# Sliding-window attention: where the softmax is scaled, and which operand stands in TensorE

## The chip, the core and the metric

One core of a Trainium2 chip runs the whole kernel as one program. TensorE (PE) multiplies, VectorE (DVE) and ScalarE (ACT) empty PSUM and do the elementwise work, GpSimd (POOL) and the queue of SyncE (SP) do little but issue transfers and small steps. The metric is the device time of one execution in microseconds (us), the median of several runs. Before the change it is 1330.35 us (three runs, 1329.46 to 1332.42).

## What is computed

A decoder trunk of two layers for 256 tokens of width 1024. Layer 0 is a gated linear recurrence and a dense feed-forward; layer 1 is attention over shared keys and values, then eight experts of which each token uses two. The change touches the attention alone:

```
scores = einsum('bnqkgd,bnskd->bnkgqs', qb, k_band) * (64 ** -0.5)
logits = where(valid, scores + bias, -inf)
m      = maximum(max(logits), sink)
p      = exp(logits - m)
probs  = p / (sum(p) + exp(sink - m))
out    = einsum('bnkgqs,bnskd->bnqkgd', probs, v_band).reshape(B, S, 16 * 64)
return out @ w_o
```

There are 16 query heads in 4 groups; the 4 heads of a group share one key head and one value head of width 64. The window is 128 tokens, and the 256 tokens are two tiles of 128: the rows of tile 0 look at the 128 keys of tile 0, those of tile 1 at all 256 keys, with the mask in the bias.

## The kernel before

Each engine has one hand-written program, and semaphores tie them together; an instruction that waits holds up all behind it on its engine. Weights of the dense parts pass through a ring of chunks: ACT rounds a chunk to `w_hi` (L597), DVE takes the rest `w_lo` (L887), and PE forms each product from three fp32r matmuls (L1413 to L1415). The experts run afterwards in a loop of 8 items on PE (L1852, L1864) whose weights come by DMA; its first buffers are loaded as chunk slots come free, and the rest is asked for (L451, L459) when the output projection of the attention has ended.

The attention stage works group by group, g = 0 to 3. Everything that PE turns or that passes from one form to another goes through the two `turn` banks of PSUM, strictly in turn: use n of a bank waits until use n-2 has been read (`turn_bank`). For a group the steps are:

- `logits(g)`, PE: the bias of the group by three 512-column matmuls (L1653), then eight score matmuls (L1708).
- `largest(g)`, DVE: three maxima over PSUM (L1222, L1224) and three small steps, which give `negm`.
- the exponentials, ACT: four of 128 columns (L809), four of 256 columns (L812), each with its row sum in `rsum`, and the sink (L815). The unscaled probabilities of a group are the 12 blocks of 128x128 of `pr`; groups take turns in two such tiles.
- `normalise(g)`, DVE: sum plus sink, reciprocal, and two multiplications that scale all 12 blocks in place (L1235, L1238).
- `turn_probs(g)`, PE: 12 transposes (L1728) in three uses u of a turn bank, each copied by DVE to `pT` (L926).
- `attend(g)`, PE: 12 fp32 matmuls in one use of a turn bank (L1740 to L1742). The values stand (128x64) and the turned probabilities stream, 128 columns. The even head of a pair writes the upper 64 partitions of the bank, the odd one the lower 64. The result has features on the partitions, as the output projection wants it.
- `att_round(g)` on ACT (L798) and `att_rest(g)` on DVE (L1242) split that bank to `ht_hi` and `ht_lo`.
- `project_out(i)`, PE: 24 fp32r matmuls of 512 columns with group i's rows of the output weights, for i = 0 and 1; `finish_out` does i = 2 and 3 bank by bank at the end.

An fp32 matmul has two records in the trace (so the 12 matmuls of `attend` are 24), a transpose and an fp32r matmul one. The order on PE is: logits(0), logits(1), then for each g: turn_probs(g), logits(g+2), attend(g); project_out(0) follows attend(2), project_out(1) stands between turn_probs(3) and attend(3), finish_out follows attend(3). On DVE: largest(0), normalise(0), largest(1), then for each g: the three copies, normalise(g+1), largest(g+2), att_rest(g); the splits of weight chunks C_O+2 and C_O+3 stand inside g = 3.

Of the kernel before, what the change touches and what calls it, by code (L numbers as in the profile page):

```python
# [8 lines left out]
P = 128  # L9
# [3 lines left out]
TT = T // P  # L13
HEADS, HD = 8, 128
CH = 64
NCH = T // CH
QH, KVH, AD = 16, 4, 64
GRP = QH // KVH
# [20 lines left out]
C_O = C_V + N_V  # L39
# [41 lines left out]
def build_program(nc, a, out):  # L81
    f32, f32r = mybir.dt.float32, mybir.dt.float32r
    i32, u32 = mybir.dt.int32, mybir.dt.uint32
    ALU, ACT, AX = mybir.AluOpType, mybir.ActivationFunctionType, mybir.AxisListType
    MUL, ADD, SUB = ALU.mult, ALU.add, ALU.subtract
# [40 lines left out]
    with ctx:  # L126
# [8 lines left out]
        h = sb(ctx, "h", [P, TT, D])  # L135
# [5 lines left out]
        xs = sb(ctx, "xs", [P, TT, D])  # L141
# [249 lines left out]
        HGRN_OUT = [[banks[2], banks[3]], [banks[0], banks[1]]]  # L391
        OUT_BANKS = [[banks[2], banks[3]], [banks[0], banks[4]]]

        TURN_ATT = 3 + HEADS + 4 + TT + 4 + 4 * KVH

        GROUPS = ((0, 0), (0, 1), (1, 0), (1, 1))
        FRESH_1 = [banks[4], banks[5], banks[2], banks[3]]
# [184 lines left out]
        def _(act):  # L582
            own = [0]
            nxt = [0]
            ta = [0]
# [207 lines left out]

            def att_round(g):

                use = ta[0] + 4 * g + 3
                act.wait_ge(turned, use + 1)
                nc.scalar.activation(ht_hi[:, 2 * g:2 * g + 2, :],  # L798
                                     turn[use % 2][:, :].rearrange("p (k t) -> p k t", k=2), ACT.Copy).then_inc(turn_hi, 1)

            for g in range(KVH):
                if g >= 2:

                    att_round(g - 2)
                act.wait_ge(negm_ready, g + 1)
                pr = prs[g % 2]
                l = LOGIT_BANKS[g % 2]
                for hh in range(GRP):
                    nc.scalar.activation(pr[:, hh, :], l[0][:, P * hh:P * hh + P], ACT.Exp, bias=negm[:, g, 0, hh:hh + 1],  # L809
                                         accum_out=rsum[:, g, 0, hh:hh + 1])  # L810
                for hh in range(GRP):
                    ins = nc.scalar.activation(pr[:, 4 + 2 * hh:6 + 2 * hh, :].rearrange("p k c -> p (k c)"),  # L812
                                               l[1 + hh % 2][:, 256 * (hh // 2):256 * (hh // 2) + 256], ACT.Exp,
                                               bias=negm[:, g, 1, hh:hh + 1], accum_out=rsum[:, g, 1, hh:hh + 1])
                nc.scalar.activation(sinkd[:, g, :, :], sinkd[:, g, :, :], ACT.Exp).then_inc(exps_ready, 1)  # L815
                if g == 0:

                    act.wait_ge(chunk_used, C_V + 1)
                    for t in range(TT):
                        nc.scalar.activation(vt[:, t, :], banks[1][:, 256 * t:256 * t + 256], ACT.Copy,  # L820
                                             scale=tok_rstd[:, 2, t:t + 1]).then_inc(kv_out, 1)
            att_round(KVH - 2)
            round_to(C_O + 3)
            att_round(KVH - 1)
            ta[0] += 4 * KVH
            assert ta[0] == TURN_ATT
            round_to(C_MOE - 1)

# [45 lines left out]
        def _(dve):  # L874
# [14 lines left out]
            def rest_to(c_last):  # L889
                while nxt[0] <= c_last:  # L890
                    c = nxt[0]
                    rest_chunk(c, c % RAW, c % SPLIT)
                    nxt[0] += 1
# [26 lines left out]
            def turn_copy(dst, part=None):  # L920

                dve.wait_ge(turned, td[0] + 1)
                src = turn[td[0] % 2][:, :] if part is None else turn[td[0] % 2][:, 0:part]
                if len(dst.shape) == 3:
                    src = src.rearrange("p (a b) -> p a b", a=dst.shape[1])
                nc.vector.tensor_copy(dst, src).then_inc(turn_free, 1)  # L926
                td[0] += 1
# [290 lines left out]
            def largest(g):  # L1218
                l = LOGIT_BANKS[g % 2]
                for i in (1, 0):  # L1220
                    dve.wait_ge(logits_full, 3 * g + 2 - i)
                    then(nc.vector.reduce_max(mx[:, g, 1, i:GRP:2], l[1 + i][:, :].rearrange("p (h k) -> p h k", h=2), axis=AX.X))  # L1222
                dve.wait_ge(logits_full, 3 * g + 3)
                then(nc.vector.reduce_max(mx[:, g, 0, :], l[0][:, :].rearrange("p (h k) -> p h k", h=4), axis=AX.X))  # L1224
                snk = sink[:, GRP * g:GRP * g + GRP].unsqueeze(1).to_broadcast([P, TT, GRP])
                then(nc.vector.tensor_tensor(mx[:, g, :, :], mx[:, g, :, :], snk, ALU.max))
                nc.vector.tensor_tensor(sinkd[:, g, :, :], snk, mx[:, g, :, :], SUB)
                nc.vector.tensor_scalar(negm[:, g, :, :], mx[:, g, :, :], -1.0, None, MUL).then_inc(negm_ready, 1)

            def normalise(g):  # L1230
                pr = prs[g % 2]
                dve.wait_ge(exps_ready, g + 1)
                then(nc.vector.tensor_tensor(rsum[:, g, :, :], rsum[:, g, :, :], sinkd[:, g, :, :], ADD))
                then(nc.vector.reciprocal(rsum[:, g, :, :], rsum[:, g, :, :]))
                nc.vector.tensor_tensor(pr[:, 0:4, :], pr[:, 0:4, :], rsum[:, g, 0, :].unsqueeze(2).to_broadcast([P, 4, P]),  # L1235
                                        MUL).then_inc(probs_ready, 1)
                p1 = pr[:, 4:12, :].rearrange("p (h k) c -> p h (k c)", k=2)
                nc.vector.tensor_tensor(p1, p1, rsum[:, g, 1, :].unsqueeze(2).to_broadcast([P, 4, 2 * P]), MUL).then_inc(probs_ready, 1)  # L1238

            def att_rest(g):  # L1240
                dve.wait_ge(turn_hi, rounded[0] + 1)
                nc.vector.tensor_tensor(ht_lo[:, 2 * g:2 * g + 2, :], turn[td[0] % 2][:, :].rearrange("p (k t) -> p k t", k=2),  # L1242
                                        plain(ht_hi[:, 2 * g:2 * g + 2, :]), SUB).then_inc(turn_free, 1)
                rounded[0] += 1
                td[0] += 1
# [2 lines left out]
            for t in range(TT):  # L1248
                turn_copy(aqT[:, 4:8, P * t:P * t + P])
            rest_to(C_O + 1)  # L1250
            normalise(0)
            largest(1)
            for g in range(KVH):
                if g == KVH - 1:
                    rest_to(C_O + 2)
                for u in range(3):
                    turn_copy(pTs[g % 2][:, 4 * u:4 * u + 4, :])
                if g + 1 < KVH:
                    normalise(g + 1)
                if g + 2 < KVH:  # L1260
                    largest(g + 2)
                if g == KVH - 1:
                    rest_to(C_O + 3)
                att_rest(g)
            rest_to(C_MOE - 1)
            add = lambda t, half: add_part(C_MOE - 1, 6, (t, half), OUT_BANKS[t][half], None)
            add(0, 0)
# [139 lines left out]
        def _(pe):  # L1407
# [315 lines left out]
            def turn_probs(g):  # L1723
                for u in range(3):
                    bank = turn_bank()
                    pe.wait_ge(probs_ready, 2 * g + (1 if u == 0 else 2))
                    for k in range(4):
                        ins = nc.tensor.transpose(bank[:, P * k:P * k + P], prs[g % 2][:, 4 * u + k, :], ident)  # L1728
                    ins.then_inc(turned, 1)
                return tp[0]  # L1730

            def attend(g, turned_by):
                pT = pTs[g % 2]
                pe.wait_ge(turn_free, turned_by)
                bank = turn_bank()
                for hh in range(GRP):
                    row, at = AD * (hh % 2), 256 * (hh // 2)
                    v = [vt[:, t, AD * g:AD * g + AD] for t in range(TT)]
                    d = bank[row:row + AD, at:at + 2 * P]
                    nc.tensor.matmul(d[:, 0:P], v[0], pT[:, hh, :], start=True, stop=True)  # L1740
                    nc.tensor.matmul(d[:, P:2 * P], v[0], pT[:, 4 + 2 * hh, :], start=True, stop=False)
                    ins = nc.tensor.matmul(d[:, P:2 * P], v[1], pT[:, 5 + 2 * hh, :], start=False, stop=True)  # L1742
                ins.then_inc(turned, 1)

            pe.wait_ge(bias_loaded, 16)
            logits(0)
            turn_queries(1)
# [4 lines left out]
            def project_out(i):  # L1752

                pe.wait_ge(turn_free, attended[i])
                to_rows(C_O + i, D, 2, 2 * i, KT, ht_hi, ht_lo, lambda t, q: OUT_BANKS[t][q][:, :], None, "parts")

            for g in range(KVH):
                turned_by = turn_probs(g)

                if g + 2 < KVH:  # L1760
                    logits(g + 2)
                if g == KVH - 1:
                    project_out(1)
                attend(g, turned_by)
                attended.append(tp[0])
                if g == KVH - 2:

                    pe.wait_ge(exps_ready, KVH)
                    project_out(0)
            assert tp[0] == TURN_ATT  # L1770

            def finish_out(t, q):
# [154 lines left out]
```

## Time and profile before

| what | value |
|---|---|
| median of the runs | 1330.35 us |
| profiled execution, its own time | 1331.27 us |
| its span, first to last instruction | 1329.3 us |
| PE busy | 1304.2 us, 98% |
| DVE busy | 360.2 us, 27% |
| ACT busy | 246.3 us, 19% |
| chain of work that ended last | PE 91%, DVE 3%, DMA 3%, ACT 2% |
| mean granted clock of TensorE | 0.995 |

The profiled execution lies 0.92 us above the median, and 1.97 us of its time lie outside the span. PE is busy nearly always, but a busy PE is not one at its peak, so what counts is how long PE takes from one step to the next: the start of a step's first record to the start of the next step's. The attention stage runs from 383 to 427 us of the span, the expert loop from 448.5 to 1321.

### The profile page before, as it was taken

What the parts mean: (1) busy time and instruction counts of PE and PEld (TensorE: products, weight loads), DVE (VectorE), ACT (ScalarE), POOL (GpSimd) and SP (SyncE); (2) the same over time, 40 slices, a digit from 0 to 9 for tenths busy, and PEclk for the clock granted to TensorE, in tenths of its full rate; (3) what the DMA queues carried; (4) which work ended last, traced back from release to release, by engine and by line L of the source; (5) the groups of instructions that cost most, each with busy time, mean ns of one, the idle gap of its engine ahead of it and who ended that gap; (6) DMA issues with size and microseconds to landing.
All of it is one profiled execution on the core that took longest, in us unless ns stands there. A gap on an engine that the chain in (4) does not pass through costs nothing.

```text
span 1329.3 us, 32581 instructions
## 1 busy us (share of the span) xinstructions
PE 1304.2 (98%) x14658; PEld 744.4 (56%) x14658; DVE 360.2 (27%) x539; ACT 246.3 (19%) x370; POOL 55.9 (4%) x50
## 2 busy tenths in 40 slices
PE   9999999999899999999999999999999999999998
PEld 8998899988767434523523533443452353353244
DVE  5875655554875411001001101101100110110111
ACT  5554544433743100000000000000000000000000
POOL 1001000000000230000000000000000000001500
PEclk9999999999999899999999999999999999999999
DMA  9867565555521897999999999999999999999996
GB/s 319 267 213 224 182 191 190 182 199 190 191 96 64 348 421 298 405 409 382 419 421 403 419 420 408 415 420 412 412 418 419 404 419 419 405 418 418 418 417 243
DMA packets 114199, 442.52 MB, mean 333 GB/s; under 512 B 9284, under 2 KB 55700, under 8 KB 83348
## 3 DMA queue, kind: packets, MB, share of 16 engines
q1 hardware_dynamic: 107904, 424.75, 81.4%
q10 hardware_dynamic: 4820, 11.53, 2.5%
q0 software_dynamic: 1344, 4.20, 0.8%
q8 instruction: 120, 1.97, 0.6%
q14 instruction: 11, 0.09, 0.0%
HBM read 434.12 MB, written 12.08 MB: 336 GB/s over the span
## 4 chain that ended last, share of the span: by engine, by line
PE 91%; DVE 3%; DMA 3%; ACT 2%; issue 1%; SPq 0%; ACTq 0%; DVEq 0%
PE bank L1852 41%; PE bank L1864 22%; PE bank L1413 8%; PE bank L1415 8%; PE bank L1414 8%; DMA raw<-in_moe_w_up 2%; DMA dn<-in_moe_w_down 1%; PE bank L1653 1%; PE bank L1571 1%; DVE w_lo L887 1%; ACT w_hi L597 0%; PE bank L1829 0%; DMA const<-in_shape_constants 0%; ACT ht_hi L625 0%; PE bank L1708 0%
## 5 line engine op out<-in xcount | busy, mean ns | idle before, releaser
L1852 PE MATMUL bank<-raw,xT 128*32 128x512 f32 (+1 forms) x4608 | 439.8, 540 | 2.8 <-DMA raw<-in_moe_w_up 2.2
L1852 PEld LDWEIGHTS bank<-raw,xT 128*32 128x32 f32 x4608 | 141.6, 110 | 294.2 <-issue 285.8
L1864 PE MATMUL bank<-dn,hidT 128*32 128x256 f32 x5376 | 291.5, 379 | 1.2 <-DMA dn<-in_moe_w_down 1.2
L1864 PEld LDWEIGHTS bank<-dn,hidT 128*32 128x32 f32 x5376 | 165.8, 110 | 127.4 <-issue 2.8
L1382 DVE TENSOR_TENSOR e_hid<-e_silu,bank 128x512 f32<-128x512 f32 (+1 forms) x48 | 26.9, 616 | 538.0 <-PE bank L1852 538.0
L887 DVE TENSOR_TENSOR w_lo<-raw,w_hi 128x2048 fp32r<-128x2048 f32 x62 | 141.7, 2291 | 102.2 <-ACT w_hi L597 102.1
L1852 PE MATMUL bank<-up_more,xT 128*32 128x384 f32 (+1 forms) x1536 | 150.0, 539 | 0.0
L1413 PE MATMUL bank<-ht_hi,w_hi 128*128 128x256 f32 x464 | 130.1, 280 | 1.5 <-DVE ht_lo L901 1.5
L1414 PE MATMUL bank<-ht_lo,w_hi 128*128 128x256 f32 x464 | 129.8, 280 | 0.0
L1415 PE MATMUL bank<-ht_hi,w_lo 128*128 128x256 f32 x464 | 129.8, 280 | 0.0
L597 ACT ACTIVATE w_hi<-raw 128x2048 fp32r<-128x2048 f32 x62 | 118.6, 1916 | 42.1 <-PE bank L1415 41.8
L860 ACT ACTIVATE e_silu<-bank 128x512 f32<-128x512 f32 (+1 forms) x48 | 22.6, 544 | 433.3 <-PE bank L1852 433.3
L1852 PEld LDWEIGHTS bank<-up_more,xT 128*32 128x32 f32 x1536 | 47.3, 110 | 97.0 <-issue 95.9
L1414 PEld LDWEIGHTS bank<-ht_lo,w_hi 128*128 128x128 f32 x464 | 88.5, 191 | 0.0
L1413 PEld LDWEIGHTS bank<-ht_hi,w_hi 128*128 128x128 f32 x464 | 87.1, 188 | 2.5 <-issue 2.4
L1415 PEld LDWEIGHTS bank<-ht_hi,w_lo 128*128 128x128 f32 x464 | 87.1, 188 | 0.0
L863 ACT ACTIVATE yb<-bank 96x512 f32<-96x512 f32 x8 | 4.7, 593 | 404.7 <-PE bank L1864 404.7
L1413 PE MATMUL bank<-w_hi,ht_hi 128*128 128x256 f32 (+1 forms) x224 | 74.8, 334 | 3.7 <-DVE ht_lo L915 1.6
L1394 DVE COPY yb<-bank 96x256 f32<-96x256 f32 x8 | 3.4, 420 | 257.8 <-PE bank L1864 257.8
L1415 PE MATMUL bank<-w_hi,ht_lo 128*128 128x256 f32 (+1 forms) x224 | 73.2, 327 | 0.0
L1414 PE MATMUL bank<-w_lo,ht_hi 128*128 128x256 f32 (+1 forms) x224 | 73.2, 327 | 0.0
L1413 PEld LDWEIGHTS bank<-w_hi,ht_hi 128*128 128x128 f32 x224 | 42.2, 188 | 9.4 <-issue 3.5
(280 smaller groups left out, 859.5 us busy)
## 6 DMA issues: line engine op xcount, KB each, us to landing
dn<-in_moe_w_down SPq DMA_DIRECT2D x112, 1024.0 KB, 12.5
raw<-in_moe_w_gate SPq DMA_DIRECT2D x48, 1024.0 KB, 14.3
raw<-in_moe_w_up SPq DMA_DIRECT2D x48, 1024.0 KB, 14.4
raw<-in_moe_w_gate SPq DMA_DIRECT2D x48, 768.0 KB, 12.1
raw<-in_moe_w_up SPq DMA_DIRECT2D x48, 768.0 KB, 8.4
up_more<-in_moe_w_gate SPq DMA_DIRECT2D x16, 1024.0 KB, 24.9
up_more<-in_moe_w_up SPq DMA_DIRECT2D x16, 1024.0 KB, 14.1
raw<-in_hgrn_w_in SPq DMA_DIRECT2D x15, 1024.0 KB, 11.7
```

Source lines behind the costliest of these rows:

```text
L597: nc.scalar.activation(w_hi[:, slot, :], raw[:, slot_raw, :], ACT.Copy).then_inc(hi_ready, 1)
L860: nc.scalar.activation(e_silu[:, j, 0:w], banks[j][:, 0:w], ACT.Silu).then_inc(e_silu_ready, 1)
L863: nc.scalar.activation(yb[:, 0:512], banks[6][0:CAP, :], ACT.Copy)
L887: nc.vector.tensor_tensor(w_lo[:, slot, :], raw[:, slot_raw, :], plain(w_hi[:, slot, :]), SUB).then_inc(split_ready, 1)
L1382: nc.vector.tensor_tensor(e_hid[:, j, 0:w], e_silu[:, j, 0:w], banks[GRPS + j][:, 0:w], MUL).then_inc(e_hid_ready, 1)
L1413: nc.tensor.matmul(dst, st[0], mv[0], start=first, stop=False)
L1414: nc.tensor.matmul(dst, st[0], mv[1], start=False, stop=False)
L1415: return nc.tensor.matmul(dst, st[1], mv[0], start=False, stop=last)
L1571: whole = lambda bank_rows, at, w, st, mv: nc.tensor.matmul(bank[bank_rows:bank_rows + CH, at:at + w], st, mv, start=True, stop=True)
L1653: nc.tensor.matmul(LOGIT_BANKS[g % 2][b][:, :], const[:, K_ANTI:K_ANTI + P], bias_rev[:, GRP * g:GRP * g + GRP, :][:, heads, 2 * P - P * ( ...
L1852: ins = nc.tensor.matmul(out_banks[j][GTOK * c:GTOK * c + GTOK, 0:w], xT[:, j, kt, :], chunk[:, c], start=kt == 0, stop=kt == KT - 1)
L1864: ins = nc.tensor.matmul(banks[6 + j // 2][GTOK * c:GTOK * c + GTOK, 256 * (j % 2):256 * (j % 2) + 256], hidT[sup][:, g, m, :], dn[:, i % ...
```

## The change

The probabilities are turned as they come from the exponential. `normalise` is gone from DVE; `sums(g)` keeps its two small steps. In `attend` the operands change places: each block of `pT` (128x128) stands and the values (64 columns) stream over it, so that tokens come out on the partitions: columns 256t + 64h of the bank hold token tile t and head h. `scale_rows(g)` on DVE reads this bank, multiplies it by the reciprocal sums and writes `xs`. A new PE step `turn_heads(g)` turns these rows, four 128x128 transposes in a turn bank of their own, and `att_round` and `att_rest` then split that bank as before. A group so takes five uses of the turn banks and not four. ACT tells PE of its exponentials in three parts (`probs_ready`). The order of the steps is written out anew on PE and DVE; project_out(0) now stands between turn_probs(3) and attend(3), and project_out(1) between turn_heads(2) and turn_heads(3).

```diff
--- before.py
+++ after.py
@@ -391,7 +391,8 @@
...
-        TURN_ATT = 3 + HEADS + 4 + TT + 4 + 4 * KVH
+        PROBS_TURN, HEADS_TURN, ROWS_TURN = (0, 4, 9, 14), (3, 8, 13, 17), (7, 12, 18, 19)
+        TURN_ATT = 3 + HEADS + 4 + TT + 4 + 5 * KVH
@@ -793,25 +794,29 @@
...
-    use = ta[0] + 4 * g + 3
+    use = ta[0] + ROWS_TURN[g]
     act.wait_ge(turned, use + 1)
...
 for g in range(KVH):
-    if g >= 2:
-
-        att_round(g - 2)
+    if g == 2:
+        act.wait_ge(turned, ta[0] + PROBS_TURN[0] + 3)
+    if g == 3:
+        att_round(0)
     act.wait_ge(negm_ready, g + 1)
...
     for hh in range(GRP):
-        nc.scalar.activation(pr[:, hh, :], l[0][:, P * hh:P * hh + P], ACT.Exp, bias=negm[:, g, 0, hh:hh + 1],
-                             accum_out=rsum[:, g, 0, hh:hh + 1])
+        ins = nc.scalar.activation(pr[:, hh, :], l[0][:, P * hh:P * hh + P], ACT.Exp, bias=negm[:, g, 0, hh:hh + 1],
+                                   accum_out=rsum[:, g, 0, hh:hh + 1])
+    ins.then_inc(probs_ready, 1)
     for hh in range(GRP):
...
                                    bias=negm[:, g, 1, hh:hh + 1], accum_out=rsum[:, g, 1, hh:hh + 1])
+        if hh % 2:
+            ins.then_inc(probs_ready, 1)
     nc.scalar.activation(sinkd[:, g, :, :], sinkd[:, g, :, :], ACT.Exp).then_inc(exps_ready, 1)
@@ -819,10 +824,11 @@
...
                                  scale=tok_rstd[:, 2, t:t + 1]).then_inc(kv_out, 1)
-att_round(KVH - 2)
+att_round(1)
 round_to(C_O + 3)
-att_round(KVH - 1)
-ta[0] += 4 * KVH
+att_round(2)
+att_round(3)
+ta[0] += 5 * KVH
 assert ta[0] == TURN_ATT
@@ -1227,15 +1233,22 @@
...
-def normalise(g):
-    pr = prs[g % 2]
+def sums(g):
     dve.wait_ge(exps_ready, g + 1)
...
     then(nc.vector.reciprocal(rsum[:, g, :, :], rsum[:, g, :, :]))
-    nc.vector.tensor_tensor(pr[:, 0:4, :], pr[:, 0:4, :], rsum[:, g, 0, :].unsqueeze(2).to_broadcast([P, 4, P]),
-                            MUL).then_inc(probs_ready, 1)
-    p1 = pr[:, 4:12, :].rearrange("p (h k) c -> p h (k c)", k=2)
-    nc.vector.tensor_tensor(p1, p1, rsum[:, g, 1, :].unsqueeze(2).to_broadcast([P, 4, 2 * P]), MUL).then_inc(probs_ready, 1)
+
+def scale_rows(g):
+
+    dve.wait_ge(turned, td[0] + 1)
+    nc.vector.tensor_tensor(xs[:, :, 256 * g:256 * g + 256].rearrange("p t (h e) -> p t h e", e=AD),
+                            turn[td[0] % 2][:, :].rearrange("p (t h e) -> p t h e", t=TT, e=AD),
+                            rsum[:, g, :, :].unsqueeze(3).to_broadcast([P, TT, GRP, AD]), MUL).then_inc(turn_free, 1)
+    td[0] += 1
+
+def turn_probs_copies(g):
+    for u in range(3):
+        turn_copy(pTs[g % 2][:, 4 * u:4 * u + 4, :])
@@ -1248,20 +1261,27 @@
...
 rest_to(C_O + 1)
-normalise(0)
 largest(1)
-for g in range(KVH):
-    if g == KVH - 1:
-        rest_to(C_O + 2)
-    for u in range(3):
-        turn_copy(pTs[g % 2][:, 4 * u:4 * u + 4, :])
-    if g + 1 < KVH:
-        normalise(g + 1)
-    if g + 2 < KVH:
-        largest(g + 2)
-    if g == KVH - 1:
-        rest_to(C_O + 3)
-    att_rest(g)
+turn_probs_copies(0)
+sums(0)
+largest(2)
+scale_rows(0)
+turn_probs_copies(1)
+sums(1)
+att_rest(0)
+largest(3)
+scale_rows(1)
+turn_probs_copies(2)
+sums(2)
+att_rest(1)
+scale_rows(2)
+turn_probs_copies(3)
+sums(3)
+rest_to(C_O + 2)
+scale_rows(3)
+att_rest(2)
+rest_to(C_O + 3)
+att_rest(3)
 rest_to(C_MOE - 1)
@@ -1723,7 +1743,7 @@
...
         bank = turn_bank()
-        pe.wait_ge(probs_ready, 2 * g + (1 if u == 0 else 2))
+        pe.wait_ge(probs_ready, 3 * g + u + 1)
         for k in range(4):
@@ -1734,14 +1754,21 @@
...
     for hh in range(GRP):
-        row, at = AD * (hh % 2), 256 * (hh // 2)
         v = [vt[:, t, AD * g:AD * g + AD] for t in range(TT)]
-        d = bank[row:row + AD, at:at + 2 * P]
-        nc.tensor.matmul(d[:, 0:P], v[0], pT[:, hh, :], start=True, stop=True)
-        nc.tensor.matmul(d[:, P:2 * P], v[0], pT[:, 4 + 2 * hh, :], start=True, stop=False)
-        ins = nc.tensor.matmul(d[:, P:2 * P], v[1], pT[:, 5 + 2 * hh, :], start=False, stop=True)
+        d0, d1 = (bank[:, 256 * t + AD * hh:256 * t + AD * hh + AD] for t in range(TT))
+        nc.tensor.matmul(d0, pT[:, hh, :], v[0], start=True, stop=True)
+        nc.tensor.matmul(d1, pT[:, 4 + 2 * hh, :], v[0], start=True, stop=False)
+        ins = nc.tensor.matmul(d1, pT[:, 5 + 2 * hh, :], v[1], start=False, stop=True)
     ins.then_inc(turned, 1)
-
+    scaled.append(tp[0])
+
+def turn_heads(g):
+
+    pe.wait_ge(turn_free, scaled[g])
+    turn_rows(lambda t: xs[:, t, :], [g])
+    attended.append(tp[0])
+
+scaled = []
 pe.wait_ge(bias_loaded, 16)
@@ -1754,19 +1781,23 @@
...
-for g in range(KVH):
-    turned_by = turn_probs(g)
-
-    if g + 2 < KVH:
-        logits(g + 2)
-    if g == KVH - 1:
-        project_out(1)
-    attend(g, turned_by)
-    attended.append(tp[0])
-    if g == KVH - 2:
-
-        pe.wait_ge(exps_ready, KVH)
-        project_out(0)
+turned_by = turn_probs(0)
+logits(2)
+attend(0, turned_by)
+turned_by = turn_probs(1)
+turn_heads(0)
+logits(3)
+attend(1, turned_by)
+turned_by = turn_probs(2)
+turn_heads(1)
+attend(2, turned_by)
+turned_by = turn_probs(3)
+pe.wait_ge(exps_ready, KVH)
+project_out(0)
+attend(3, turned_by)
+turn_heads(2)
+project_out(1)
+turn_heads(3)
 assert tp[0] == TURN_ATT
```

## Rows read from the trace of the kernel before

**Rows 1.** Stretches: each engine's busy us, PEclk, DMA share, GB/s.

```profile
core 0: us, PE busy (x) PEld busy (x) DVE busy (x) ACT busy (x) POOL busy (x), PEclk, DMA share, GB/s
383.00:427.00 44.00, 38.96 (x255) 29.43 (x254) 29.04 (x49) 16.38 (x57) 0.00 (x0) 0.96 0.14 49
...
440.00:449.00 9.00, 8.07 (x62) 4.17 (x65) 4.57 (x25) 0.06 (x1) 0.00 (x0) 0.50 1.01 424
449.00:1321.00 872.00, 868.59 (x11522) 354.65 (x11514) 73.80 (x150) 33.79 (x73) 40.25 (x28) 1.00 0.99 405
```

**Rows 2.** Chain that ended last, one item of the expert loop: start, us, what.

```profile
882.94 72.16 PE bank L1852 x768
955.10 36.26 PE bank L1864 x672
```

**Rows 3.** Timeline of SP's queue: start, us, issued transfers.

```profile
436.10 0.81 SPq L451 DMA_DIRECT2D up_more<-in_moe_w_gate  x2
```

**Rows 4.** Waits from 383 to 427 us: total us, times, longest us.

```profile
PE bank L1728 <- DVE pT L926: 2.2, 2, 1.8
PE bank L1728 <- DVE ht_lo L1242: 2.1, 2, 1.2
...
PE bank L1740 <- DVE pT L926: 0.8, 1, 0.8
```

**Rows 5.** Timeline of PE: start, us, line, out<-in, records [idle before <-releaser].

```profile
390.62 0.43 PE L1740 MATMUL bank<-pT,vt 128*64 128x128 f32 x2
...
392.35 0.66 PE L1728 MATMUL bank<-const,pr 128*128 128x128 f32 x4
394.25 1.25 PE L1728 MATMUL bank<-const,pr 128*128 128x128 f32 x8 [1.24 <-DVE ht_lo L1242]
395.34 2.74 PE L1653 MATMUL bank<-bias_rev,const 128*128 128x512 f32 x6
...
399.52 0.43 PE L1740 MATMUL bank<-pT,vt 128*64 128x128 f32 x2
...
401.25 0.66 PE L1728 MATMUL bank<-const,pr 128*128 128x128 f32 x4
...
404.77 0.43 PE L1740 MATMUL bank<-pT,vt 128*64 128x128 f32 x2 [0.78 <-DVE pT L926]
...
407.61 0.80 PE L1413 MATMUL bank<-w_hi,ht_hi 128*128 128x512 f32 x1
...
413.80 1.03 PE L1728 MATMUL bank<-const,pr 128*128 128x128 f32 x8
...
415.59 0.48 PE L1413 MATMUL bank<-w_hi,ht_hi 128*128 128x512 f32 x1
...
421.28 0.43 PE L1740 MATMUL bank<-pT,vt 128*64 128x128 f32 x2
...
423.01 0.50 PE L1413 MATMUL bank<-w_hi,ht_hi 128*128 128x512 f32 x1
```

**Rows 6.** Stretches of 1 us, PE alone: busy, PEclk, DMA share, GB/s.

```profile
406.00:407.00 1.00, 1.00 (x12) 0.50 0.06 16
```

**Rows 7.** Timeline of PE, the router's matmuls: 128x128 stands, 8 columns stream.

```profile
436.84 2.78 PE L1800 MATMUL bank<-router,hnT 128*128 128x8 f32 x24
```

**Rows 8.** Timeline of DVE: start, us, line, operation, operands [idle before].

```profile
371.39 0.69 DVE L1205 TENSOR_TENSOR xs<-bank,rstd 128x512 f32<-128x512 f32 x1
...
389.24 0.69 DVE L1235 TENSOR_TENSOR pr<-pr,rsum 128x512 f32<-128x512 f32 x1
389.85 1.22 DVE L1238 TENSOR_TENSOR pr<-pr,rsum 128x1024 f32<-128x1024 f32 x1
...
393.51 0.69 DVE L1242 TENSOR_TENSOR ht_lo<-bank,ht_hi 128x512 fp32r<-128x512 f32 x1
394.11 0.68 DVE L926 COPY pT<-bank 128x512 f32<-128x512 f32 x1
394.94 0.69 DVE L926 COPY pT<-bank 128x512 f32<-128x512 f32 x1 [0.15 <-PE bank L1728]
```

**Rows 9.** Timeline of ACT: the last exponential of group 3.

```profile
405.12 0.24 ACT L815 ACTIVATE sinkd<-sinkd 128x8 f32<-128x8 f32 x1
```

## Prediction

> **What bounds the kernel now.** I read the stretches first. From 449 to 1321 us, the expert loop, PE is busy 868.59 of 872 us at full clock with the DMA engines at 0.99 [rows 1]; one item of the loop is 72.16 + 36.26 = 108.4 us of the chain with PE in every part of it [rows 2]. The two are nearly tied there, but neither has slack towards the attention: the loop's bulk transfers are asked for at 436.10 us, when the output projection has ended [rows 3], and PE enters the loop behind the same projection. So whatever the attention stage gains or loses shifts both by the same amount, and the whole of it shows in the time. The question is only how long PE takes from 383 to about 427 us.
>
> In that stage PE is busy 38.96 of 44 us [rows 1], so 5.04 us are idle. The waits say to whom: 2.2 us to the copies of `pT` before transposes, 2.1 us to `att_rest`, 0.8 us to a copy before `attend` [rows 4]. That is all that a lighter DVE can give back. The largest piece, 1.8 us, lies in turn_probs(0), where the copy stands behind largest(1); the change leaves this order as it is, so that piece stays. The reader is to see in the timeline of PE that every other step stands directly behind the one before.
>
> **The clock.** From about 405.3 to 408.6 us the granted clock is 0.50, the lower of the two levels, 1.2 GHz [rows 6]; before it fell PE had mostly turned blocks and waited. What it costs is read from equal steps: `attend` takes 392.35 - 390.62 = 1.73 us, and also 1.73 us at 399.52 and at 421.28, but 407.61 - 404.77 = 2.84 us for group 2; project_out(0) takes 413.80 - 407.61 = 6.19 us, project_out(1) 421.28 - 415.59 = 5.69 us [rows 5]. That is 1.1 + 0.5 = 1.6 us.
>
> **Parts with next to no price.** `normalise` gives DVE back 1.8 us a group (389.24 to 389.85 + 1.22) and `scale_rows` takes 0.6 to 0.7 us of it, as a step on a PSUM bank times a broadcast column does [rows 8]. DVE was late for PE only through largest(1) and `att_rest`, so its 4.5 us of lighter work buy only what the walk below shows. The exponentials of group 3 end at 405.4 us now [rows 9]; PE will want them after 408.6, so the finer `probs_ready` buys nothing. `largest` and the split chunks keep their distance: the split of C_O+3 moves behind att_rest(2), 4 us before finish_out needs it, and the queue of SP behind it loads into an idle stretch (DMA share 0.14 [rows 1]).
>
> **The attend step, the term that decides.** Now 24 records in 1.73 us, 72 ns each [rows 5]; the even and odd heads go to different halves of the array's columns. After the change 24 records each put a full 128x128 block in place for 64 columns. No row has that shape; the ends are these. Upper: the router's matmuls stand 128x128 and stream only 8 columns, and 24 records take 2.78 us, of which the last is its own latency of 0.26: (2.78 - 0.26)/23 = 110 ns [rows 7]. There is nothing to stream, so 110 ns is the standing block itself. Lower: if the block could be hidden, 64 columns at half of what the 128 of today's form cost per lane (two lanes, 2 x 55 ns a record) give 55 ns, 1.3 us in all. The router row has the very stationary shape and is nearest, so I take 24 x 0.110 = 2.64 and 0.06 for changing over: 2.70 us. It is +0.97 us for each of four groups, +3.9.
>
> The Trainium skill speaks against this edit: TensorEngine Tiling (Array Packing), section Performance Considerations, advises for a streamed side of 64 or less to swap the operands and tile the columns, which is the form of before, not the one after. TensorE: Matmul & The Clock Gate, section LDWEIGHTS, says that loading takes time by the number of columns, P/1.2 ns, so an estimate of 107 ns for 128; by that the attend step would be 2.6 us, and the 110 ns of the router row agree.
>
> **The walk.** Hand-overs, from group 1 of before: DVE step to PE's next use of its bank 0.74 us (393.51 to 394.25), four transposes with copy behind them 0.69 (394.25 to 394.94), DVE step to next 0.60 (393.51 to 394.11) [rows 5, 8]; four transposes 0.45.
> - Group 1: the first four transposes may start at once; the second four wait for scale_rows(0), which starts 0.2 us after attend's last start plus its latency; then the third, then turn_heads(0), which waits for the copy of the second: 0.92 + 0.69 + 0.74 + 0.48 = 2.83 us until logits(3). Before: 395.34 - 392.35 = 2.99. So -0.2, with the new transposes in it.
> - Group 2 in the same way, ending on the last copy: 2.94 us until attend(2). Before: 404.77 - 401.25 = 3.52. -0.6.
> - Group 3: 0.92 + 0.60 + 0.46 = 1.98 us until the projection; before 415.59 - 413.80 = 1.79. +0.2.
> - turn_heads(2) and (3) stand bare between PE's other work: 2 x 0.44 = +0.9. Their split banks follow at the same distance as now behind attend(3); I add 0.1 for the wait before i = 3.
>
> Sum: 3.9 - 0.2 - 0.6 + 0.2 + 0.9 + 0.1 = +4.3 us, at the same clock on both sides. So the change turns 2 us of waiting into work, and adds more work than that. Against the profiled execution it is 1331.27 + 4.3 = 1335.6; this lies 0.92 above the median, so the forecast for the median is 1330.35 + 4.3 = 1334.6 us.
>
> **The rivals.**
> - The low clock does not come back. For it: group 2's waits shrink. Against: in the new order 64-column records keep the array streaming only half of the time, and three groups of transposes follow each. 1334.6 - 1.6 = 1333.0.
> - It comes back and stays twice as long, since what follows is thin too: +1.6, 1336.3.
> - The standing block is partly hidden: a record of 72 ns, the step stays at 1.73, 1334.6 - 3.9 = 1330.7. Against it stands [rows 7].
> - Faster: records priced by their 64 columns, 55 ns, `attend` 1.3 us (-0.4 each, -1.6 in all), and the clock stays up: 0.4 for the rest of the walk, - 1.6 - 1.6 = -2.8, 1327.5. Its place is the attend step. It decides for faster by over 0.2% where that step takes less than 1.36 us with the clock up; with the clock as before the step would have to be under 0.96. A rule of the skill goes this way: the tiling page's Key Properties say that changing the tiling mode drains the array, and before it changes twice a group. The row shows 1.73 - 1.31 = 0.42 us beyond 24 x 55 ns, which may be that drain; by it alone each step would win at most 0.4.
> - The DVE relief reaches the path after all (the 1.8 us of turn_probs(0) goes): 1332.8. Only if the copies passed largest(1); the written order excludes it.
>
> **How the numbers follow.** A measurement of this kernel can tell about 0.2% from no change, 2.7 us: 1327.7 to 1333.0. Chances: forecast 0.48; clock stays up 0.20; two low stretches 0.12; block partly hidden or some of DVE's relief seen 0.14; faster 0.06. Slower by over 0.2% is the first, the third and part of the second, 0.66; within, 0.27; faster, 0.07. The range leaves out the fast rival and half of the partly hidden one below, and what goes beyond two low stretches above: 1330.6 to 1337.2.
>
> **What would show it.** In the profile after: 24 records of `attend` at 110 ns, 2.6 to 2.8 us a step (0.055 or 0.072 would sink the forecast); four transposes a group more; waits of PE on `xs` of 0.4 us a group in place of those on `ht_lo`; the 1.8 us before turn_probs(0)'s third part still there; project_out(1) at 5.7 us; the loop's items at 108.4 us and its first transfers as much later than 436.1 as the whole kernel is. A low clock at another length than 3.3 us moves the sum by half of the difference.

## The result and the profile after

The change makes the kernel slower by 0.2 to 0.35%: 1332.26 us median (12 runs, 1329.62 to 1334.91) against 1329.38 for the kernel before on the same chip (12 runs). The medians lie 2.9 us or 0.22% apart; the ratio on record for the same runs, with its 95% interval, is 1.0035 (1.0022 to 1.0048). A second comparison later gave 1332.11 against 1329.33 and 1.0020 (1.0007 to 1.0032). The profiled execution took 1334.33 us, its span 1332.5.

The first view is the head of the page of the kernel after: DVE does 5 us less than before, PE 4 us more, and the share that PE is busy is what it was.

```profile
span 1332.5 us, 32618 instructions
...
PE 1308.3 (98%) x14674; PEld 748.9 (56%) x14674; DVE 355.4 (27%) x535; ACT 246.3 (18%) x370; POOL 56.0 (4%) x50
```

The timeline of PE through the stage answers to [rows 5] (start, us, line, operands, records, idle before). One goes from the start of one step to that of the next: the transposes are L1748, attend L1759 to L1761, the bias matmuls L1673, the turned heads L1452, the projection L1433.

```profile
382.11 1.09 PE L1748 MATMUL bank<-const,pr 128*128 128x128 f32 x8
...
389.72 0.43 PE L1759 MATMUL bank<-vt,pT 128*128 128x64 f32 x2
...
392.45 0.61 PE L1748 MATMUL bank<-const,pr 128*128 128x128 f32 x4
393.39 1.25 PE L1748 MATMUL bank<-const,pr 128*128 128x128 f32 x8 [0.34 <-DVE xs L1244]
394.93 0.63 PE L1452 MATMUL bank<-const,xs 128*128 128x128 f32 x4 [0.28 <-DVE pT L932]
395.39 2.74 PE L1673 MATMUL bank<-bias_rev,const 128*128 128x512 f32 x6
...
405.37 0.41 PE L1759 MATMUL bank<-vt,pT 128*128 128x64 f32 x2
...
408.07 0.60 PE L1748 MATMUL bank<-const,pr 128*128 128x128 f32 x4
...
424.21 0.60 PE L1452 MATMUL bank<-const,xs 128*128 128x128 f32 x4
424.56 0.48 PE L1433 MATMUL bank<-w_hi,ht_hi 128*128 128x512 f32 x1
```

An attend step is 392.45 - 389.72 = 2.73 us, and 2.70 for group 2, where the step of before is 1.73 at full clock. The waits of PE in the stage are these (total us, times, longest us); they answer to [rows 4]:

```profile
PE bank L1748 <- DVE pT L932: 1.8, 1, 1.8
PE bank L1748 <- DVE xs L1244: 1.0, 3, 0.3
PE bank L1452 <- DVE pT L932: 0.6, 2, 0.3
```

So 3.4 us of waiting are left of 5.1; the 1.8 us of turn_probs(0) stand untouched.

**Comparing stages, not traces.** The stage did not begin at the same time in any two executions: turn_probs(0) started between 381.1 and 386.7 us in the twelve traces read here, and at 382.11 and 384.56 us in the two of the changed kernel. So I take the stage's own length, from the start of turn_probs(0) to the start of finish_out. It is 424.56 - 382.11 = 42.45 us after, and 423.01 - 383.02 = 39.99 before, of which 1.6 are low clock. Behind the stage both kernels run alike: the bulk transfers are asked for at 437.82 us and not at 436.10 [rows 3], 1.72 us later, and the last addition of the output starts 1.70 us later (1327.80 against 1326.10). The spans differ by more, 3.2 us: the other 1.5 us lie behind that addition, where the span ends 4.7 us after its start in this trace and 3.2 in the first of before. That tail does not go with the kernel: in the second traces it is 3.1 us after the change and 3.6 before it. An item of the expert loop takes 72.16 + 36.26 us in the chain of both [rows 2].

### The profile page after: what moved, and what is told of

Same layout as the page of the kernel before. It is cut to its first block, busy times and chain, and to the rows that moved or that the text cites. A ratio compares the mean times of both kernels' runs of the same rounds, so it can differ in the third digit from the quotient of the medians.

```text
span 1332.5 us, 32618 instructions
## 1 busy us (share of the span) xinstructions
PE 1308.3 (98%) x14674; PEld 748.9 (56%) x14674; DVE 355.4 (27%) x535; ACT 246.3 (18%) x370; POOL 56.0 (4%) x50
## 4 chain that ended last, share of the span: by engine, by line
PE 91%; DMA 3%; DVE 3%; ACT 2%; issue 1%; SPq 0%; ACTq 0%; DVEq 0%
PE bank L1883 41%; PE bank L1895 22%; PE bank L1433 8%; PE bank L1435 8%; PE bank L1434 8%; DMA raw<-in_moe_w_up 2%; DMA dn<-in_moe_w_down 1%; PE bank L1673 1%; PE bank L1591 1%; DVE w_lo L893 1%; ACT w_hi L598 0%; PE bank L1728 0%; PE bank L1860 0%; DMA const<-in_shape_constants 0%; ACT ht_hi L626 0%
## 5 line engine op out<-in xcount | busy, mean ns | idle before, releaser
L1433 PE MATMUL bank<-ht_hi,w_hi 128*128 128x256 f32 x464 | 130.2, 281 | 1.5 <-DVE ht_lo L907 1.5
L1433 PEld LDWEIGHTS bank<-ht_hi,w_hi 128*128 128x128 f32 x464 | 87.1, 188 | 2.5 <-issue 2.4
L1433 PE MATMUL bank<-w_hi,ht_hi 128*128 128x256 f32 (+1 forms) x224 | 74.5, 332 | 3.7 <-DVE ht_lo L921 1.6
L1433 PEld LDWEIGHTS bank<-w_hi,ht_hi 128*128 128x128 f32 x224 | 42.1, 188 | 9.0 <-issue 3.0
```

Source lines behind the costliest of these rows:

```text
L1433: nc.tensor.matmul(dst, st[0], mv[0], start=first, stop=False)
```

## The experiments

Every time is compared with the kernel before on the same chip. The short diffs leave out what only carries the edit.

**Is it the operands? Values put to stand again, in the new order (x1).**

```diff
-    d0, d1 = (bank[:, 256 * t + AD * hh:256 * t + AD * hh + AD] for t in range(TT))
-    nc.tensor.matmul(d0, pT[:, hh, :], v[0], start=True, stop=True)
+    d = bank[row:row + AD, at:at + 2 * P]
+    nc.tensor.matmul(d[:, 0:P], v[0], pT[:, hh, :], start=True, stop=True)
...
```

> The changed kernel with the operands of attend put back alone: the values stand (128x64) and the turned probabilities stream (128 columns); everything around it is as after the change. This leaves the scaling and the turning of the rows to work on the wrong layout, so only the time is meant. My theory (the standing 128x128 block costs 110 ns a record): each attend step goes from 2.69 back to 1.73 us, the stage ends 3.8 us earlier, and the time is 3.8 us below the changed kernel, so 0 to +0.5 us against the kernel before. Rival (the added steps turn_heads and the new order carry the loss): the step may get shorter, but waits take the place, and the time stays 3 us or more above before.

Measured: 1330.01 us median, ratio 1.0012 (1.0000 to 1.0023). The attend steps are back at 1.73 and 1.74 us. The stage takes 420.59 - 381.08 = 39.51 us, 2.9 less than the changed kernel and not 3.8, because a part came back as waiting. Its timeline of PE:

```profile
388.69 0.43 PE L1760 MATMUL bank<-pT,vt 128*64 128x128 f32 x2
...
390.43 0.66 PE L1748 MATMUL bank<-const,pr 128*128 128x128 f32 x4
391.70 1.25 PE L1748 MATMUL bank<-const,pr 128*128 128x128 f32 x8 [0.62 <-DVE xs L1244]
```

The wait for `scale_rows` is 0.62 us here and 0.34 after the change. Still, most of the loss goes with the operands. What is left, 39.51 against 38.29 (below), is the rest of the change: the turned heads, less what the shorter waits give back.

**The operands exchanged alone, in the kernel before (x2)** (the same edit the other way round).

> The kernel before with the operands of attend exchanged alone: the probabilities stand and the values stream; the split of the heads then works on the wrong layout, so only the time is meant. My theory: +0.97 us a step, +3.9 us in all against before, seen as 110 ns a record. Rival (the change of tiling mode that is saved pays for it): each step gains up to 0.4 us on the way in and out, +2.3 us in all. Rival (64 columns stream in half of the time): no loss, -1.6 us.

Measured: 1332.83 us, ratio 1.0022 (1.0009 to 1.0036). The stage takes 429.76 - 386.36 = 43.40 us in this trace, but a stretch of low clock lies on project_out(0), which takes 6.98 us and not 5.61, and on the end of attend(2) (2.90, not 2.73). Without these 1.54 us the stage is 41.86, 3.6 us above before at full clock. The saved changes of tiling mode did not pay as the rival had it, with up to 0.4 us a step: the step is 2.73 us, as in the changed kernel, start to start:

```profile
393.97 0.43 PE L1739 MATMUL bank<-vt,pT 128*128 128x64 f32 x2
394.24 0.39 PE L1740 MATMUL bank<-vt,pT 128*128 128x64 f32 x2
...
396.48 0.39 PE L1741 MATMUL bank<-vt,pT 128*128 128x64 f32 x2
396.70 0.50 PE L1728 MATMUL bank<-const,pr 128*128 128x128 f32 x3
```

Between the second pair and the last are 20 records in 2.24 us: 112 ns each.

**Is it the standing block? Twice the columns over it (x3).**

```diff
-    v = [vt[:, t, AD * g:AD * g + AD] for t in range(TT)]
+    v = [vt[:, t, AD * g_:AD * g_ + 2 * AD] for t in range(TT)]
```

> The changed kernel with 128 columns of values streamed over each standing block and not 64, into overlapping halves of the bank (group 3 uses group 2's values), so twice the streamed work and a wrong output. My theory (the standing block sets 110 ns, the stream is hidden behind it): nothing changes, each step stays at 2.7 us and the time within 1 us of the changed kernel. Rival (record time is block plus stream, or the stream alone): a record takes 130 to 160 ns and the time is 2 to 5 us above the changed kernel.

Measured: 1333.5 us, ratio 1.0029 (1.0014 to 1.0044), and a stage of 42.67 us against 42.45. The rows of the same 20 records, now of 128 columns:

```profile
393.10 0.39 PE L1761 MATMUL bank<-vt,pT 128*128 128x128 f32 x2
...
395.34 0.39 PE L1762 MATMUL bank<-vt,pT 128*128 128x128 f32 x2
```

2.24 us again, 112 ns a record. With 8 columns it is 110 ns [rows 7], with 64 and with 128 it is 112. So over a standing 128x128 block of fp32 the streamed columns are free up to 128, but for 0.05 us a step (2.78 against 2.73). That the floor of 110 ns is the block going into place is the likely reading, and not shown: no run changed the size of the block alone. The form of before differs in two things, a block half as wide and two column halves at work at once (in its trace records of two heads interleave: L1741 starts at 390.89, L1740 at 390.90), and the runs exchange both together. Its 24 records in 1.73 us only exclude that every fp32 record has to follow the one before it by 110 ns.

**What was the relief of VectorE worth (x4)?** The two multiplications of `normalise` left out:

```diff
-    nc.vector.tensor_tensor(pr[:, 0:4, :], pr[:, 0:4, :], rsum[...].to_broadcast([P, 4, P]), MUL)...
-    nc.vector.tensor_tensor(p1, p1, rsum[...].to_broadcast([P, 4, 2 * P]), MUL)...
```

> The kernel before with the two multiplications of normalise left out (the probabilities stay unscaled), the most that the relief of VectorE can give without any new work. My theory: the wait before turn_probs(0)'s third part stays at 1.8 us, since it is behind largest(1); the waits on att_rest shrink by about 0.5 us in group 1 and little in group 2; in all -0.5 to -1.5 us against before, and at most 1.6 more where the low clock stays away. Rival (VectorE was what held the stage): -3 us or more.

The whole time (1437.4 us) says nothing here: unscaled attention sends tokens to other experts, and the loop ran one item more, 108.4 us. The stage can be read: 37.97 us, against 38.29 for before at full clock. Its waits of PE are 2.3 us on the copies, 1.6 on `att_rest` and 0.8 before attend(2); of [rows 4] only the second has lost anything, 0.5 us. So in this order of work the relief is worth 0.3 us, and the range that I gave began too high.

**The kernel before, once more (x5).**

> The kernel before, unchanged, for a second trace. My theory (the stretch of low clock in the attention stage comes by chance of the execution, not by the kernel): the steps from turn_probs(0) to finish_out have the same lengths except where the clock is low, which lies elsewhere or is not there; at full clock throughout the stage takes 38.4 us where the first trace has 40.0. Rival (it belongs to the order of before): the low clock falls on attend(2) again and the stage takes 40.0 us.

Measured: 1329.38 us. The clock is full through the whole stage, and its length is 420.73 - 382.44 = 38.29 us. The waits of PE are those of [rows 4] to a tenth. So 38.29 is the length to compare with, and the 1.6 us of the first trace were the clock. Where the second trace differs:

```profile
404.00:408.00 4.00, 3.82 (x33) 1.00 0.01 4
```

(stretch, PE busy, PEclk, DMA share, GB/s), against 0.50 in [rows 6]. So the low clock of the stage does not belong to its order; it comes in some executions. Nor is it the only one. Read in slices of 1 us, the first trace of before is low for 3.4 us here and for 10.2 us from 439 us on, between the stage and the expert loop; this second one for 10.2 us from 436 us on.

**The turned heads (x6).** One transpose of the four in each turn_heads:

> The changed kernel with one transpose in each turn_heads and not four, so that most of the heads' rows are not turned and the output is wrong. My theory (each transpose costs 0.11 us of PE in a row, and the waits for the banks in front of it stay): turn_heads(2) and (3) take 0.1 us and not 0.4; groups 1 and 2 get shorter by the same 0.3 each, 1.3 us in all. Rival (PE waits there anyway): the groups keep their length and only the two bare steps get shorter, 0.6 us.

Measured: 1334.79 us in the one run, and a stage of 41.47 us, 0.98 less than 42.45. Group 1 and the two bare steps lose 0.33 us each, so a transpose left out is worth 0.11. Group 2 loses nothing: it is 3.08 us from its first transposes to attend(2), as with all four (3.07). The row shows why; attend(2) now waits for the copy that the transposes had covered:

```profile
406.28 0.41 PE L1759 MATMUL bank<-vt,pT 128*128 128x64 f32 x2 [0.30 <-DVE pT L932]
```

So my 1.3 was 0.3 too much, and the rival's 0.6 too little.

**Filling the waits instead.** If PE's row of steps sets the stage, work that is there already can go into the 5.04 us of waiting of the kernel before. First the bias matmuls alone (x7):

```diff
 def turn_probs(g):
     for u in range(3):
+        if u == (2 if g == 0 else 1) and g + 2 < KVH:
+            logit_biases(g + 2)
```

> The kernel before with the bias matmuls of logits(2) moved in front of the third part of turn_probs(0), and those of logits(3) in front of the second part of turn_probs(1), where PE waits 1.84 and 1.24 us; nothing is added. My theory (PE's row of steps sets the stage): the first wait is filled and is won in full, 1.8 us; of the second about half a microsecond stays since att_rest(0) then stands behind largest(2) and so the win is 0.6; in all -2.4 us, -4 where the low clock stays away too. Rival (VectorE sets the stage, whatever PE does first): the waits move to turn_probs(1) and (2), and less than 1 us is won.

Measured: 1331.3 us, ratio 1.0023 (1.0009 to 1.0037): slower. This theory fell. The first wait did go, but the rows show a new one:

```profile
397.92 1.25 PE L1734 MATMUL bank<-const,pr 128*128 128x128 f32 x8 [0.72 <-DVE ht_lo L1242]
...
406.21 1.82 PE L1734 MATMUL bank<-const,pr 128*128 128x128 f32 x8 [3.21 <-DVE ht_lo L1242]
```

PE reaches turn_probs(2) earlier, and VectorE, with normalise(2) and largest(3) still ahead of att_rest(1), does not: 0.83 us of wait became 3.21. A low clock followed it (0.50 from 408 to 412 us), and over its 12 runs the mean granted clock is 0.9935 where before has 0.9962. The stage of this trace is 427.50 - 386.70 = 40.80 us. Of that 2.7 us are low clock (attend(2) takes 3.24 us and not 1.73, project_out(0) 6.23 and not 5.61, the last eight transposes of group 2 with their wait 2.61 and not 2.03), so at full clock it would be 38.1: the filling won 0.2 us, and the time was lost to the clock.

**More filler (x8).** As x7, and the first three output blocks of project_out(0) go between the first and second part of turn_probs(2), the fourth ahead of attend(2), and the first of project_out(1) into turn_probs(3). On VectorE largest(3) goes ahead of normalise(2).

> As x7, and three of the four output blocks of project_out(0) stand between the first and the second part of turn_probs(2), the fourth in front of attend(2), the first block of project_out(1) between the first and the second part of turn_probs(3), and largest(3) goes before normalise(2). My theory: of the 5.04 us of waiting in the stage at most 1.5 stay, so -3.5 us against before at the same clock and up to -5 where the low clock stays away. Rival (VectorE sets the stage): no better than x7.

Measured: 1330.36 us, ratio 1.0009 (0.9999 to 1.0020), a stage of 38.02 us at full clock. I had expected at most 1.5 us of waits to stay; 5.4 us are there, so nothing is won and this theory fell too. The waits had moved, to places that can be named:

```profile
401.16 0.63 PE L1742 MATMUL bank<-const,pr 128*128 128x128 f32 x4 [1.66 <-DVE pr L1235]
...
415.34 0.66 PE L1742 MATMUL bank<-const,pr 128*128 128x128 f32 x4 [3.01 <-DVE pT L926]
```

The 1.66 us is the swap on DVE: the multiplication comes behind largest(3). The 3.01 us is a split of a weight chunk that nobody needs yet, in front of the copies; the timeline of DVE has it waiting for ScalarE and then at work while PE waits:

```profile
412.39 2.29 DVE L887 TENSOR_TENSOR w_lo<-raw,w_hi 128x2048 fp32r<-128x2048 f32 x1 [1.11 <-ACT w_hi L597]
414.60 1.28 DVE L926 COPY pT<-bank 128x512 f32<-128x512 f32 x2
```

**With both orders set (x9).**

```diff
     for u in range(3):
         turn_copy(pTs[g % 2][:, 4 * u:4 * u + 4, :])
     if g + 1 < KVH:
         normalise(g + 1)
-    if g + 2 < KVH:
-        largest(g + 2)
+    if g == 0:
+        largest(2)
+    att_rest(g) if g < KVH - 1 else rest_to(C_O + 3)
+    if g == 1:
+        largest(3)
```

> As x8, with the order of VectorE set by what its trace showed: the split of weight chunk C_O+2 goes behind the copies of turn_probs(3) (it made PE wait 3.01 us there), normalise(2) goes before largest(3) and att_rest(1) too (1.66 us), the fourth block of project_out(0) stands behind attend(2), and project_out(1) is whole between turn_probs(3) and attend(3). Nothing is computed otherwise. My theory (stage length at full clock plus what the low clock costs is the whole difference in time): the stage takes 34.7 to 35.7 us where before takes 38.3, and the time is 2.5 to 4 us below before, less what a lower mean clock costs. Rival (VectorE and ScalarE set the stage whatever the order): the waits move on, and the stage stays above 37.5 us.

Measured: 1325.2 us median against 1329.33, ratio 0.9969 (0.9954 to 0.9984), the best kernel here. The stage takes 419.17 - 384.46 = 34.71 us. Its first and last step, and what is left of PE's waits:

```profile
384.46 1.09 PE L1737 MATMUL bank<-const,pr 128*128 128x128 f32 x8
...
419.17 0.50 PE L1412 MATMUL bank<-w_hi,ht_hi 128*128 128x512 f32 x1
...
PE bank L1749 <- DVE pT L926: 0.9, 1, 0.9
PE bank L1737 <- DVE ht_lo L1242: 0.7, 1, 0.7
PE bank L1737 <- DVE pT L926: 0.2, 1, 0.2
```

VectorE multiplies all that it multiplied before. Its relief was not needed; its order was, once PE had something to do in the meantime. The 3.6 us of stage are seen in the time, 4.1 us between the medians, of which a part may be the clock: the runs' mean is 0.9968, and 0.9957 for before beside them.

**The changed kernel, once more (x10).**

> The changed kernel once more, beside before on the same chip. My theory: the stage takes 42.4 us at full clock against 38.3 of before, and the time is 2 to 5 us above before. Rival (a low clock of before was saved and pays a part): the mean clock of the changed kernel's runs is above that of before, and the ratio is under 1.002.

Measured: 1332.11 us, ratio 1.0020 (1.0007 to 1.0032); the stage takes 427.01 - 384.56 = 42.45 us, to 0.01 us that of the first trace. The rival has a part in it: the mean granted clock of its 10 runs is 0.9979, that of the 22 runs of before beside it 0.9957. Its bound for the ratio, under 1.002, is just missed.

## Why the prediction was right, and where it was off

The forecast was +4.3 us. The stage at full clock grew by 42.45 - 38.29 = 4.16 us, and 0.2 us come behind the start of finish_out (the end, below): 4.3 in all. The first comparison's ratio stands for 4.7 us (2.9 to 6.4), the second's for 2.7 (0.9 to 4.3). So the mechanism was right and nearly every term with it; the assumption of an equal clock on both sides was not.

- **What bounds the kernel.** Right. The loop's items kept their 108.4 us, and the transfers and the end moved together by 1.7 us in the pair of first traces.
- **The attend step, +3.9.** Right: 2.73, 2.73, 2.70 and 2.63 us in the second trace, +3.9 against four times 1.73. I took the value from the router's matmuls, which have the same standing block; 110 ns there, 112 here, and the run with twice the columns showed that the stream is hidden. That it is the standing block itself, as I wrote, stays likely and not shown. The 0.4 us a step that the rival of the drain allowed off this price did not appear; whether the 0.42 us that the old step has beyond 24 x 55 ns are a drain stays open.
- **Group 1, -0.2.** 2.94 us against 2.99, so -0.05. I had 2.83: from the start of the copy that turn_heads waits for (394.09 us) to turn_heads are 0.84 us, and I had 0.74.
- **Group 2, -0.6.** 3.07 against 3.51, -0.4, for the same reason.
- **Group 3, +0.2.** 1.96 against 1.80, +0.2.
- **The bare heads, +0.9.** 0.36 and 0.35, so +0.7. Three of the four transposes are worth 0.32 us (x6), 0.11 each, and the first adds only 0.04.
- **The projection steps, no term.** project_out(0) and (1) take 5.60 us each, where the second trace of before has 5.61 and 5.68: -0.1. I had named 5.7 for project_out(1); the difference lies between its last product and attend(3), 0.33 us before and 0.23 after.
- **The end, +0.1.** +0.2: the i = 3 products start 0.41 us after the last record before them, where 0.23 is their pace.
- **The hidden parts** cost nothing, as said. The last split of a weight chunk began at 420.13 us, behind att_rest(2), and finish_out started its matmuls at 424.56 without a wait for it.
- **The clock, at the same cost on both sides.** This step failed. The low stretch appeared in the stage in one of two traces of before, and in none of the two of the changed kernel. Over all runs whose clock was listed the mean is 0.9960 for before (71 runs) and 0.9972 for after (22: 0.9966 in the first comparison, 0.9979 in the second). In before, the four runs with 0.999 took 1326.0 us in the mean, the nine with 0.994 took 1332.0: about 1.2 us for each thousandth. By that, an estimate, the changed kernel gets some 1.4 us back, and of 4.3 us about 2.9 remain, which is what lies between the medians (2.9 and 2.8). The same runs can be compared at equal clock: at 0.996 six runs of the changed kernel are 3.3 us above 22 of before, at 0.997 nine are 4.9 above 21, at 0.999 six are 5.4 above four; with the one at 0.995, and weighted by the runs of the changed kernel, 4.6 us. The intervals alone would not show it, since 4.3 us lies inside the first and at the edge of the second. In kind this is the rival "the low clock does not come back", worked out at -1.6. It also accounts for the 1334.6 being 2.3 us too high: 1.4 of it is this, 1.0 the median of before, 1330.35 in three runs and 1329.38 in twelve.
- **Where the clock was low.** The rival looked only at the stage, and that is the smaller part. Both traces of before are low for 10.2 us between the stage and the expert loop; the changed kernel is low for 10.2 us there in its first trace (from 441 us), but in its second for 3.4 us (from 444) and for 3.4 us at 147, far ahead of anything that was changed. Why its mean clock is higher I have not shown. In the stage its waits after the first are 0.34 us or less, where before has 1.24, 0.83 and 0.78, but four traces with low stretches in four places don't say that this is the cause.
- **The relief of VectorE.** Together with the new order of steps it took PE's waits from 5.1 to 3.4 us, as the walk had it. Alone it bought 0.3. The order of the work, PE's and its own, was worth ten times that, which the waits did not show, since each wait that was filled brought another engine's queue into view.

## What to carry to other kernels

Before exchanging the operands of a matmul, price the standing side: 24 records over full 128x128 fp32 blocks took 2.7 to 2.8 us whether 8, 64 or 128 columns streamed, and the half-width form that runs two heads side by side in the array took 1.73. If an engine waits in a row of short steps, look first for work of its own that is ready and independent, and move it in; then look at which queue the next wait ends in and put that queue's order right, before taking work away from it. Compare such small changes by the length of the stage in several traces, for the rest of the kernel moves by more than they are worth.

## What was not expected of the hardware

- The stage began anywhere from 381.1 to 386.7 us in twelve traces, and 2.5 us apart in the two of the changed kernel; its length, at full clock, was 42.45 us in both of these.
- The clock falls in some executions and not in others of the same program: at 405 us in one trace of before, not at all in the other's stage; for 10.2 us behind the stage in one trace of the changed kernel and for 3.4 in the other. Runs of before with a mean clock of 0.994 are 6 us longer than those with 0.999.
- With one wait of 3.21 us in place of shorter ones the share of low clock went up: 0.9935 on the average of 12 runs, against 0.9962 of the runs of before beside them. That the wait is the cause was not tried by itself; x8 has one of 3.01 us, and 0.9955.
